# Issuing the three products of a split matmul for both token halves together, on alternating banks

## The reference

```
proj = x @ W_in      # GLA q/k/v, gate rank, out-gate, MLA latents, rope key, two merge gates
y_gla = W_gla_o( swish(og) * RMSNorm_head( GLA_chunked(q, k, v, gate) ) )   # 4 heads
y_mla = W_mla_o( causal softmax attention with compressed q/kv )            # 8 heads
h   = LN(alpha * x + W_out( sigmoid(g_a) * y_gla + sigmoid(g_b) * y_mla ))
[a, b] = causal depthwise conv3(h @ W_up)      # width 2 x 2816
out = LN(alpha * h + W_down( silu(a) * b ))
```

## Time and profile before

| what | value |
|---|---|
| median of 3 runs | 2084.63 us (2084.44 to 2085.03) |
| span of the profiled execution | 2082.5 us |
| what lies around the span, against the median of the runs | 2.1 us |
| TensorE busy, matmuls | 1940.5 us (93%), 9,676 of them |
| weight loads | 1629.1 us (78%), 9,676 of them |
| VectorE, ScalarE, GpSimd busy | 964.6, 514.3, 515.8 us |
| mean granted TensorE clock | 0.97 |

### The profile page before, as it was taken

One profiled execution on the slowest core, in us unless ns is written; L12 is line 12 of the kernel. 1 busy time (PEld: TensorE's weight loads), 2 busy tenths in 40 slices (PEclk: granted clock), 3 DMA queues, 4 the chain that ended last, 5 costly groups with the idle time before them and its releaser, 6 DMA issues.

```text
span 2082.5 us, 23389 instructions
## 1 busy us (share of the span) xinstructions
PE 1940.5 (93%) x9676; PEld 1629.1 (78%) x9676; DVE 964.6 (46%) x1428; ACT 514.3 (25%) x931; POOL 515.8 (25%) x201
## 2 busy tenths in 40 slices
PE   6999999998999987989988989799999999899995
PEld 5888888887889966777767877588888888788884
DVE  1224233323212175666674534666654555433546
ACT  2323132412200333334441101312111111211112
POOL 2222222122232210010111223032322323133344
PEclk9999999999999998999999999799999999999998
DMA  5112112123542131112132331122221111311212
GB/s 165 41 41 63 59 33 69 41 97 111 171 134 84 34 100 58 35 34 72 46 102 92 131 142 41 31 76 76 61 61 41 51 51 31 109 43 51 71 41 81
DMA packets 143108, 149.56 MB, mean 72 GB/s; under 512 B 14172, under 2 KB 110604, under 8 KB 143004
## 3 DMA queue, kind: packets, MB, share of 16 engines
q1 hardware_dynamic: 103200, 79.77, 12.8%
q10 hardware_dynamic: 39804, 68.31, 9.5%
HBM read 115.03 MB, written 33.03 MB: 71 GB/s over the span
## 4 chain that ended last, share of the span: by engine, by line
PE 82%; DVE 12%; ACT 3%; ACTq 1%; issue 1%; DMA 0%; POOLq 0%; POOL 0%; DVEq 0%
PE psum_all L506 25%; PE psum_all L508 24%; PE psum_all L507 24%; DVE nmax L1066 2%; DVE p_sb L1077 2%; DVE pT_lo L847 1%; ACT p_sb L1486 1%; PE psum_all L545 1%; PE psum_all L732 1%; PE psum_all L734 1%; PE psum_all L733 1%; PE psum_all L583 1%; PE psum_all L579 1%; PE psum_all L581 1%; DVE psum_all L1065 1%
## 5 line engine op out<-in xcount | busy, mean ns | idle before, releaser
L487 POOL CAST w_hi<-w_raw 128x2048 fp32r<-128x2048 f32 (+6 forms) x89 | 140.5, 1579 | 1534.1 <-PE psum_all L508 1516.8
L489 POOL TENSOR_TENSOR w_lo<-w_raw,w_hi 128x2048 fp32r<-128x2048 f32 (+6 forms) x89 | 354.6, 3985 | 7.1
L506 PE MATMUL psum_all<-hT_hi,w_hi 128*128 128x512 f32 x704 | 276.4, 393 | 10.2 <-DVE hT_lo L847 10.2
L507 PE MATMUL psum_all<-hT_lo,w_hi 128*128 128x512 f32 x704 | 275.7, 392 | 0.0
L508 PE MATMUL psum_all<-hT_hi,w_lo 128*128 128x512 f32 x704 | 275.6, 391 | 0.0
L506 PE MATMUL psum_all<-xT_hi,w_hi 128*128 128x512 f32 (+1 forms) x528 | 209.5, 397 | 1.4 <-DVE xT_lo L847 1.4
L508 PE MATMUL psum_all<-xT_hi,w_lo 128*128 128x512 f32 (+1 forms) x528 | 206.4, 391 | 0.0
L507 PE MATMUL psum_all<-xT_lo,w_hi 128*128 128x512 f32 (+1 forms) x528 | 206.3, 391 | 0.0
L506 PEld LDWEIGHTS psum_all<-hT_hi,w_hi 128*128 128x128 f32 x704 | 133.3, 189 | 38.5 <-DVE hT_lo L847 10.8
L507 PEld LDWEIGHTS psum_all<-hT_lo,w_hi 128*128 128x128 f32 x704 | 133.4, 190 | 27.9
L508 PEld LDWEIGHTS psum_all<-hT_hi,w_lo 128*128 128x128 f32 x704 | 133.3, 189 | 27.8
(11 more groups left out here) (334 smaller groups left out, 3606.5 us busy)
## 6 DMA issues: line engine op xcount, KB each, us to landing
w_raw<-in_w_up_dram SPq DMA_DIRECT2D x44, 512.0 KB, 4.7
w_raw<-in_w_in_dram SPq DMA_DIRECT2D x16, 1024.0 KB, 5.2
w_raw<-in_w_down_dram SPq DMA_DIRECT2D x22, 512.0 KB, 3.7
x_tok<-in_x_dram SPq DMA_DIRECT2D x8, 512.0 KB, 7.4
w_raw<-in_w_in_dram SPq DMA_DIRECT2D x8, 512.0 KB, 5.2
d_og<-oT_st ACTq DMA_DIRECT2D x16, 256.0 KB, 2.1
d_sga<-sig ACTq DMA_DIRECT2D x16, 256.0 KB, 2.3
w_raw<-in_w_gla_o_dram SPq DMA_DIRECT2D x4, 1024.0 KB, 5.3
```

What stands on the lines that cost most here:

```text
L487: nc.gpsimd.tensor_copy(w_hi[n % 2][:, 0:w], w_raw[n % 2][:, 0:w]).then_inc(w_high, 1)
L489: nc.gpsimd.tensor_tensor(w_lo[n % 2][:, 0:w], w_raw[n % 2][:, 0:w], w_hi[n % 2][:, 0:w].bitcast(F32), ALU.subtract).then_inc(w_split, 1)
L506: pe.matmul(out_ap, ah, bh, start=start and i == 0, stop=False)
L507: pe.matmul(out_ap, ah, bl, start=False, stop=False)
```

## The change

A new function, `split3_halves`, takes two banks and both halves of the moving operand. For each k tile it issues w_hi·x_hi into bank 0 and bank 1, w_hi·x_lo into bank 0 and bank 1, w_lo·x_hi into bank 0 and bank 1. `features` uses it for a tile's two groups, having waited for both banks; both groups end one matmul apart. The single groups inside the GLA heads stay as they are, under the name `feature_one`. In w_up, slots 1 to 21 do their gate tile for both halves and then their value tile for both halves (slot 0 keeps its order), and ScalarE's waits count the groups in the new order.

```
-            def features(kind, name, th, tl, js=range(4)):
+            def split3_halves(outs, terms):
+                for i, (wh, wl, halves) in enumerate(terms):
+                    first, last = i == 0, i == len(terms) - 1
+                    for o, (xh, xl) in zip(outs, halves):
+                        pe.matmul(o, wh, xh, start=first, stop=False)
+                    for o, (xh, xl) in zip(outs, halves):
+                        pe.matmul(o, wh, xl, start=False, stop=False)
+                    ends = [pe.matmul(o, wl, xh, start=False, stop=last) for o, (xh, xl) in zip(outs, halves)]
+                return ends
...
+            def features(kind, name, th, tl):
                 n = need(name)
-                for j in js:
-                    feature_group(kind + (j,), n, j // 2, j % 2, th, tl)
+                for tile in range(2):
+                    kinds = [kind + (2 * tile,), kind + (2 * tile + 1,)]
+                    free(kinds[0])
+                    free(kinds[1])
+                    for end in split3_halves([bank(kinds[0]), bank(kinds[1])],
+                                             [(w_part(n, k, tile * P, P), w_part(n, k, tile * P, P, True), halves_of(th, tl, k)) for k in range(KT)]):
+                        end.then_inc(mm, 1)
...
             for i in range(1, FT):
                 if i >= 2:
                     pe.wait_ge(sm["up_c"], 4 * (i - 1))
-                for half in range(2):
-                    for part in range(2):
-                        up_group(i, half, part)
+                n = need(("up", i))
+                for part in range(2):
+                    b = 4 * (i % 2) + 2 * part
+                    for end in split3_halves([psum[b], psum[b + 1]],
+                                             [(w_part(n, k, part * P, P), w_part(n, k, part * P, P, True), halves_of(hT_hi, hT_lo, k)) for k in range(KT)]):
+                        end.then_inc(sm["up_mm"], 1)
...
-                        ac.wait_ge(sm["up_mm"], 4 * i + 2 * half + part + 1)
+                        ac.wait_ge(sm["up_mm"], 4 * i + (2 * part + half if i else n * 2 + part) + 1)
```

More of the change, by code:

```diff
@@ L523, in feature_group, with halves_of, feature_one @@
                 return last
-            def features(kind, name, th, tl, js=range(4)):
-                n = need(name)
-                for j in js:
-                    feature_group(kind + (j,), n, j // 2, j % 2, th, tl)
+            def split3_halves(outs, terms):
[7 more added lines that the diff above has]
+                return ends
+            def halves_of(th, tl, k):
+                return [(th[:, k, half * HALF:(half + 1) * HALF], tl[:, k, half * HALF:(half + 1) * HALF]) for half in range(2)]
+            def features(kind, name, th, tl):
+                n = need(name)
+                for tile in range(2):
[5 more added lines that the diff above has]
+                        end.then_inc(mm, 1)
+            def feature_one(kind, name, th, tl, j):
+                n = need(name)
+                feature_group(kind + (j,), n, j // 2, j % 2, th, tl)
             def v_groups(h, js=range(4)):
@@ L619, in _ @@
                     if last_head:
-                        features(("ga", t // 4), ("ga", t // 4), xT_hi, xT_lo, [t % 4])
+                        feature_one(("ga", t // 4), ("ga", t // 4), xT_hi, xT_lo, t % 4)
                     elif t < 4:
-                        features(("og", h + 1), ("og", h + 1), xT_hi, xT_lo, [t])
+                        feature_one(("og", h + 1), ("og", h + 1), xT_hi, xT_lo, t)
                     else:
```

## The result

| | executions | median, us | mean, us | range, us |
|---|---|---|---|---|
| before, first measurement | 4 | 2084.59 | 2084.7 | 2084.44 to 2085.03 |
| changed, first measurement | 4 | 2096.74 | 2096.8 | 2095.56 to 2098.17 |
| before, all measurements of this study | 110 | 2090.6 | 2089.3 | 2082.31 to 2097.21 |
| changed, all | 10 | 2097.1 | 2097.7 | 2095.56 to 2103.89 |

The changed kernel is slower: ratio 1.0054, 95% interval 1.004 to 1.0069, 12.1 us between the medians. The forecast was 2092.5 in a range of 2088.4 to 2097.5, so the sign and the range held and the size was 4.2 us short. The lower half of the table came with the experiments: the four executions of the kernel before in the first measurement were all in the lowest of several bunches of times, and the mean over all executions moves by 8.4 us (standard error 0.9), not 12.1.

A forecast was written before the change was run, and what follows sets the result against it. TensorE bounds it (93% of the span): matmul count times distance, plus gaps. Terms 4.6 + 0.6 + 0.8 + 1.0 + 0.9 = 7.9 us lift the span from 2082.5 to 2090.4, with 2.1 around it 2092.5; range 2088.4 to 2097.5.

The forecast's parts named there:

- The pace: 3,456 reordered matmuls in features and w_up: distance from start to start stays 226.5 ns, so zero change.
- Rival (1): At 2,304 same-tile, other-bank steps each matmul gets up to 14 ns shorter, giving 2060 us; 6 in 100.
- From w_up to w_down: After w_up's last slot both value tiles come last, so w_down starts later: +4.6 us, bounds 4.0 and 5.2.
- The clock behind it: After the longer gap before w_down, more loss at half clock: +0.6 us, bounds -0.7 and +1.1.
- Within w_up: nothing: Between w_up slots the later convolved results stay covered by some 10 us, so no cost.
- `gb` 3 to `cT`: Two sigmoids with stores, not one, precede the first `cT_hi` on ScalarE: +0.8 us, bounds 0.5 and 1.0.
- `oT` to `gb`: In three heads `gb` waits for two read-outs of `oT`, not one: +1.0 us, bounds 0.7 and 1.2.
- `ga` 3 to `glao`: Later `ga` read-outs delay the `oT` splits and reloads that `glao` awaits: +0.9 us, bounds 0 and 3.3.
- The step that failed: Final sum: adds 7.9 us to the profiled span 2082.5, then 2.1 around it, giving 2092.5 against median 2084.63.
- (2): Rival: handoffs mostly covered, w_up's tail 4.0 us, clock returns sooner, `gb` and `glao` don't wait: 2088.4 us; 12 in 100.
- (3): Rival: last `oT` split slips behind GpSimd's next subtraction, `glao` waits some 8 us: 2101.6 us; 5 in 100.
- (4): Rival: each of the 3,456 reordered matmul steps is dearer by 1 ns: 2096 us; 3 in 100.

The follow-up runs named there:

- w_up alone: Only w_up slots 1 to 21 in the new order, feature slots as in the kernel before: mean 2095.4 +- 1.7 us, ratio 1.0024 to the kernel before.
- the longer filling: More small matmuls in eight long TensorE waits than a first filling; medians 2074.49 us added to the kernel before, 2082.38 added to the changed kernel.
- the handoffs undone: Changed kernel with w_up's last slot and the ga and gb slots in the old order: mean 2090.0 us, ratio 0.9991; long waits filled, median 2074.55.

## Why the prediction was right, and where it was off

**The pace.** Right: 226.4 ns on both sides, and 0.06 us between the medians over 2,784 paired matmuls once the long waits are filled. Rival (1) has nothing. The reason given, that each matmul brings its own load so that a repeated tile saves none, agrees with 672 loads for 672 matmuls of line 532. No run leaves a load out, so that this is the reason is argued and not shown, and what the 14 ns above the bare streaming are was not tried. The Trainium skill's "load once and matmul repeatedly" ("TensorE: Matmul & The Clock Gate", step 1 of "Step-by-step: what each phase is for") is not what happens in this kernel: its trace has 9,676 loads for 9,676 matmuls. The 25 us that the prediction estimated from the Trainium skill's gap did not come.

**From w_up to w_down.** Right to 0.1 us: 4.6 forecast, 11.56 - 6.96 = 4.60 measured, with the operations in the order given and GpSimd holding the first product. The last slot in the old order removes the gap's growth.

**The clock behind it.** 0.6 forecast; this trace has 5.2 us of half clock behind the restart against 2.9, a loss of 2.6 against 1.5, so 1.1, my upper bound. The step "For a gap of 11.6 us in place of 7 I take the middle" was somewhat low; the trace of w_up alone loses 1.0 us more there too.

**Within w_up: nothing.** Right; no wait of TensorE in 432 us.

**`gb` 3 to `cT`, `oT` to `gb`, `ga` 3 to `glao`.** 0.8, 1.0 and 0.9 forecast; 0.75, 1.2 (just above its upper bound) and 0.6 measured. The last of these hangs on reloads and was 0.4 to 0.8 in other traces. The chain of copies ran as listed: split 3 caught by GpSimd, copy 5 waiting for its reload, the last split 1.3 us before `glao`. `ga` 2 behind the last head's `oT`, which I had put down as free, is so by luck: in both first traces the transposes ahead of it run at half clock, and it follows them after 0.07 us. In the changed kernel with the longer filling they run at full clock, and it follows after 0.44 us in place of 0.03.

**The step that failed** is "The profiled span of 2082.5 becomes 2090.4; with the 2.1 us around it, 2092.5 against the median 2084.63". It takes the span of one execution, and the agreement of three, for the kernel's time. The granted clock falls in other places from one execution to the next, and 2084.6 is its cheapest bunch; with that base in the first measurement, and ordinary executions on the changed side, 7.9 us of cost showed as 12.1. Over all executions the cost is 8.4 +- 0.9, beside each other on one chip 9.8 +- 1.5, and with the longer filling 7.8 between medians (9.5 +- 1.1 between means). The terms were right and the base was not. That the range held was partly luck: its top came from bounds that do not contain this spread, while single executions of the kernel before reach 2097.2 and of the changed one 2103.9.

**The other rivals.** (2) The handoffs are not covered: those outside w_up's end make 2.6 us in the trace. (3) The last split of `oT` ends at 555.6, ahead of GpSimd's next subtraction at 557.47. (4) No step is dearer by 1 ns.

Left open: why the bunches are where they are, the high executions of w_up alone, and the four of the changed kernel with the longer filling. Open too is why the first four executions of the kernel before fell into one bunch. 32 of the other 106 are in it, so if executions were independent, four of four would come about once in 120 times (an estimate); whether the chip or the batch had a part was not tried.

## What to carry to other kernels

Where groups of matmuls are followed by a read-out that something waits for, ending two groups together moves a whole read-out behind the last matmul; look at the last group before each change of stage, not at the stage. Reordering float32 matmuls of 128x512 for a shared stationary tile or for alternating banks bought nothing here, where each matmul brings its own load. Before believing a difference of half a per cent between kernels whose TensorE pauses often, run the unchanged kernel a few dozen times, or fill the long waits in both and compare then.

## What the runs showed of the hardware

One program's time was near 2084.5 us (36 executions of 110), between 2090 and 2094 (46) or near 2097 (12), with 16 elsewhere, and two traces of it differ in which of its 2 us waits are followed by a half-clock stretch. Half clock is not a loss everywhere: in the last steps of attention (1081.0 to 1084.2 us) the kernel before runs nine matmuls at half clock and waits 1.1 us from the last start before its next product; the kernel with the handoffs undone runs the same nine at full clock and waits 2.8. Both wait for the same tile of VectorE. Small float32 matmuls in the long waits, results unused, kept the granted clock at 1.00 around w_out, where it had been 0.57, took 15 us (0.7%) off the kernel before and narrowed its range from 15 us to 1.7 (5 executions); the changed kernel with the same filling still has a range of 9.8. The VectorE product of `up_g` and `up_v`, both in SBUF, took 0.69 us alone and up to 5.1 where it overlapped GpSimd's subtraction. The Trainium skill ("SBUF — State Buffer", "Who interferes with whom") says that a VectorE instruction with two SBUF inputs contends with a GpSimd instruction that reads SBUF. All traces here agree: of the 44 products of each, the 21 or 22 without such an overlap took 0.69 us.
